# A two-block model step on one core: weights stored as 8 KB rows, TensorE started on zeros, and a re-ordered front

## The reference, cut to what matters

```
h    = rmsnorm(x, g_mix);  proj = h @ w_in              # 1024 x 8208: fox q,k,v | fox_f | sc | dn q,k,v | dn_b | dn_a | z | gates
fox  : 8 heads of 64, q,k normed;  s = q@k^T/8 + cum_f[query] - cum_f[key], causal, softmax, @ v
       cum_f = cumsum(log_sigmoid(fox_f + b_fox_f))
sc   : sb * conv3(sc * sv)
dn   : silu(conv4(dn_qkv)), gated delta rule in chunks of 64, rmsnorm, * silu(z)
x   += (sum_n (y_n @ w_branch[n]) * sigmoid(gate_n)) @ w_o
x   += (silu(conv3(rmsnorm(x) @ w_up)[gate]) * [val]) @ w_down
x   += sigmoid(rmsnorm(x) @ w_ple_gate) * (p @ w_ple)
# second block
x   += concat(diff_attention, pool_mixer) @ ab_w_out ;  x += relu(rmsnorm(x) @ ffn_w1)^2 @ ffn_w2
x   += gated linear attention (gla)                  ;  x += the same kind of ffn again
out  = rmsnorm(x, norm_final)
```

## Time and profile before

| | |
|---|---|
| median of 3 runs | 1150.38 us (1149.55 to 1152.32) |
| the profiled execution | 1149.01 us, of which the span from first to last instruction is 1147.3 |
| PE busy | 1106.8 us, 96% |
| PE weight loads | 980.0 us, 85% |
| DVE, ACT, POOL busy | 67%, 48%, 4% |
| mean granted TensorE clock | 0.990 of full |
| DMA | 185.07 MB, mean 161 GB/s |

### The profile page before, as it was taken

How to read it: one execution, slowest core, us unless ns; L and a number is a source line. 1 busy time by engine, 2 the same in 40 slices (tenths; PEclk the granted TensorE clock), 3 DMA queues, 4 the chain that set the end, 5 groups by cost and what they waited for, 6 DMA issues and landing times.

```text
span 1147.3 us, 17690 instructions
## 1 busy us (share of the span) xinstructions
PE 1106.8 (96%) x7526; PEld 980.0 (85%) x7526; DVE 774.3 (67%) x946; ACT 552.2 (48%) x645; POOL 48.9 (4%) x116
## 2 busy tenths in 40 slices
PE   7899999999999999999998999999999999999996
PEld 6797988998889999998787788888888898888885
DVE  4567688554467998887677576555667876656554
ACT  5457474334446443444664454444454665444442
POOL 8100000000000000000003200000000000000000
PEclk9899899999999999999999999999999999999999
DMA  6776675663355555554553356555635435565551
GB/s 237 185 166 118 111 145 124 138 111 109 103 193 166 189 186 185 191 190 156 182 164 135 120 172 194 186 185 191 197 126 167 129 137 175 183 201 184 184 183 55
DMA packets 128511, 185.07 MB, mean 161 GB/s; under 512 B 6932, under 2 KB 104225, under 8 KB 128434
## 3 DMA queue, kind: packets, MB, share of 16 engines
q1 hardware_dynamic: 123200, 182.46, 53.6%
q10 hardware_dynamic: 4690, 1.36, 0.5%
q0 software_dynamic: 544, 0.13, 0.1%
HBM read 182.89 MB, written 1.05 MB: 160 GB/s over the span
## 4 chain that ended last, share of the span: by engine, by line
PE 82%; DVE 10%; ACT 3%; issue 2%; DMA 2%; SPq 0%; DVEq 0%; ACTq 0%
PE ps L2053 11%; PE ps L2055 10%; PE ps L2068 10%; PE ps L1994 10%; PE ps L2033 9%; PE ps L2039 8%; PE ps L2034 8%; PE ps L2000 5%; DVE low L1344 2%; DMA raw<-in_w_in 2%; DVE arena L1504 1%; PE ps L2083 1%; PE ps L2259 1%; ACT arena L1067 1%; ACT whi L947 0%
## 5 line engine op out<-in xcount | busy, mean ns | idle before, releaser
L947 ACT ACTIVATE whi<-raw 128x2048 fp32r<-128x2048 f32 x170 | 324.0, 1911 | 328.2 <-PE ps L2068 150.7
L1344 DVE TENSOR_TENSOR low<-raw,whi 128x2048 fp32r<-128x2048 f32 x170 | 389.6, 2295 | 56.9 <-ACT whi L947 54.1
L2033 PE MATMUL ps<-hboth,whi 128*128 128x256 f32 x944 | 237.8, 290 | 1.1 <-ACT conv L1043 1.1
L2034 PE MATMUL ps<-hboth,whi 128*128 128x256 f32 x944 | 232.6, 284 | 0.0
L2033 PEld LDWEIGHTS ps<-hboth,whi 128*128 128x128 f32 x944 | 181.6, 192 | 5.9 <-issue 2.9
L2034 PEld LDWEIGHTS ps<-hboth,whi 128*128 128x128 f32 x944 | 182.1, 193 | 0.9 <-issue 0.5
L2053 PE MATMUL ps<-whi,ahi 128*128 128x512 f32 x416 | 164.0, 394 | 4.4 <-issue 2.0
L2055 PE MATMUL ps<-whi,alo 128*128 128x512 f32 x416 | 162.6, 391 | 0.0
L2039 PE MATMUL ps<-hboth,low 128*128 128x256 f32 x944 | 133.3, 284 | 0.3 <-DVE low L1344 0.3
L1994 PE MATMUL ps<-hboth,whi 128*128 128x512 f32 x512 | 128.1, 392 | 0.0
L2039 PEld LDWEIGHTS ps<-hboth,low 128*128 128x128 f32 x944 | 122.6, 193 | 0.5 <-DVE low L1344 0.5
(11 more groups left out here) (393 smaller groups left out, 1222.6 us busy)
## 6 DMA issues: line engine op xcount, KB each, us to landing
raw<-in_ffn_w SPq DMA_DIRECT2D x64, 1024.0 KB, 5.2
raw<-in_w_in SPq DMA_DIRECT2D x30, 1024.0 KB, 10.1
raw<-in_w_up SPq DMA_DIRECT2D x22, 1024.0 KB, 5.1
raw<-in_gla_w_in SPq DMA_DIRECT2D x12, 1024.0 KB, 5.3
raw<-in_w_down SPq DMA_DIRECT2D x11, 1024.0 KB, 4.9
raw<-in_ab_w_in SPq DMA_DIRECT2D x8, 1024.0 KB, 5.2
raw<-in_w_branch SPq DMA_DIRECT2D x6, 1024.0 KB, 5.1
raw<-in_w_o SPq DMA_DIRECT2D x4, 1024.0 KB, 4.9
```

The source lines that it names most:

```text
L947: act.activation(whi[:, u % SPLIT, :], raw[:, u % RAW, :], ACT.Copy).then_inc(sem("hi_done"), 1)
L1344: dve.tensor_tensor(wlo[:, u % RAW, :], raw[:, u % RAW, :], whi[:, u % SPLIT, :].bitcast(F32), ALU.subtract).then_inc(sem("lo_done"), 1)
L2033: pe.matmul(out, wh, hi[:, k0 + k, :], start=opens and k == 0, stop=False, skip_group_check=True)
L2034: pe.matmul(out, wh, lo[:, k0 + k, :], start=False, stop=False, skip_group_check=True)
```

## The change

1. **Layout.** The host now stores every unit as one block of 128 rows of 8 KB (`laid_out`), so a load is 128 rows of 8 KB, contiguous in HBM; the pieces of unit 0 are rows of 2 KB, those of unit 1 rows of 4 KB. SBUF contents are the same.
2. **Parameters.** All per-channel parameters, `g_mix` among them, come as columns in one DMA (128 x 264 f32) on the ACT queue at the start. The 17 POOL DMAs, the memset of their rows, the transposes L2095 and L2109 and the DVE copies out of PSUM are gone. The bias, `dt_bias` and `a_log` rows are one DMA, the small weights another (5 before). p is stored transposed, so the 4 transposes of `ple_p` are gone.
3. **Zeros.** DVE's first instruction clears a 128x128 tile, and PE then multiplies it by itself 12 times (f32) into bank 7 before it waits for anything else.
4. **Gate sums by tile.** `fcum` of the first tile is the gate times (triangle minus 1), that of the second the gate times the triangle: both tiles are counted from the border between them, and the product L2143 is gone. Only differences of the sums are used.
5. **Order.** In the front, `fox(1, 1)` comes before `fox(2, 0)`, the dn units come as 0, 2, 1, 5, 4, 3, and some gates change places; the three tables `steps_at` change. `load_params` issues its 2 DMAs one unit later than before.

```
-    fox(0, 0) fox(0, 1) fox(1, 0) fox(2, 0) dn(0) fox(2, 1) fox(1, 1) dn(5) dn(4) dn(2) dn(1) dn(3)
+    fox(0, 0) fox(0, 1) fox(1, 0) fox(1, 1) fox(2, 0) dn(0) fox(2, 1) dn(2) dn(1) dn(5) dn(4) dn(3)
```

```
-        0: [("load_params", 0)],
-        4: [("load_params", 1)],
-        7: [("params",)],
+        2: [("load_params", 0)],
+        5: [("load_params", 1)],
+        10: [("params",), ("small_split",)],
...
-        15: [("att_norm", 1, 5), ("ab_sum", 0), ("att_turn", 1, 5), ("ab_turn", 0), ("att_values", 1, 4), ("att_values", 1, 5)],
+        15: [("att_norm", 1, 5), ("ab_sum", 0), ("att_turn", 1, 5), ("att_values", 1, 4), ("ab_turn", 0)],
+        16: [("att_values", 1, 5), ("ab_sum", 1)],
...
-        19: [("gla_pairs", 8), ("gla_mask", 8), ("gla_values", 0), ("gla_values", 1), ("gla_sum", 0), ("gla_sum", 1)],
+        19: [("gla_pairs", 7), ("gla_mask", 7), ("gla_pairs", 8), ("gla_mask", 8)],
+        20: [("gla_values", 0), ("gla_sum", 0), ("gla_values", 1)],
...
-                dst = raw[:, u % RAW, :].rearrange("p (k n) -> p k n", k=src.shape[1])
+                src, dst = units[u]["src"], raw[:, u % RAW, :]
...
+    def units(w, rows, cols):
+        r, c = w.shape[0] // rows, w.shape[1] // cols
+        w = w.reshape(r, rows // P, P, c, cols).transpose(0, 3, 2, 1, 4)
+        return w.reshape(r * c, P, UNIT)
...
-                    if t:
-                        lf = zz[:, 3, 0, 4 * b:4 * b + 4].unsqueeze(2).to_broadcast([P, 4, P])
-                        pe.matmul(out, ones[:, :], lf, start=True, stop=False)
-                    pe.matmul(out, ones[:, :], fcum[:, t, 4 * b:4 * b + 4, :], start=t == 0, stop=True)\
+                    pe.matmul(out, ones[:, :], fcum[:, t, 4 * b:4 * b + 4, :], start=True, stop=True)\
...
-                    dve.tensor_tensor(fcum[:, t], wide(tri[:, :].unsqueeze(1), [FH, P]),
-                                      wide(zz[:, 3, t, 0:FH].unsqueeze(2), [FH, P]), ALU.mult)\
+                    dve.scalar_tensor_tensor(out=fcum[:, t], in0=wide(tri[:, :].unsqueeze(1), [FH, P]),
+                                             scalar=-1.0 if t == 0 else 0.0,
+                                             in1=wide(zz[:, 3, t, 0:FH].unsqueeze(2), [FH, P]), op0=ALU.add, op1=ALU.mult)\
...
+            dve.memset(idle, 0.0).then_inc(sem("idle_made"), 1)
...
+            pe.wait_ge(sem("idle_made"), 1)
+            for _ in range(12):
+                pe.matmul(ps[:, 7, 0:P], idle, idle, start=True, stop=True)
```

More of the change, by code:

```diff
@@ L79, in add, with unit_c, unit_w, unit_b @@
         return len(units) - 1
-    def unit_c(w, c0, act, needs):
+    def unit_c(w, act, needs):
         before = [u for u in units if u["kind"] in "CB"]
         bank = 5 if before and before[-1]["kind"] == "C" and before[-1]["bank"] == 4 else 4
[L84 to L97, removed]
+        return add("C", w, act, needs, [f"c{bank}"], bank=bank)
+    def unit_w(w, bank, act, needs):
+        return add("C", w, act, needs, ["c4" if bank == 4 else "c5"], bank=bank, wide=True)
+    def unit_b(w, act, k0, needs, bank, groups):
+        return add("B", w, act, needs, groups, bank=bank, k0=k0)
+    def unit_d(w, act, k0, first, last, needs):
+        return add("D", w, act, needs, ["g0", "g1"], k0=k0, first=first,
                    last=last)
@@ L243, in sc @@
     def sc(e, part):
-        u = unit_c(w_in, o_sc + part * SW + 256 * e, "h", h_ready)
+        u = unit_c(a["w_sc"][SW // 256 * part + e], "h", h_ready)
         if part == 1:
@@ L262, in build @@
     fox(1, 0)
+    fox(1, 1)
     fox(2, 0)
@@ L265, in build @@
     fox(2, 1)
-    fox(1, 1)
+    dn(2)
+    dn(1)
     dn(5)
     dn(4)
-    dn(2)
-    dn(1)
     dn(3)
@@ L279, in build @@
     sc(1, 0)
+    gate(1)
     gate(0)
-    gate(1)
     branch(0, 0, "fox_lo")
@@ L288, in build @@
     branch(1, 0, "sc_lo")
+    gate(6)
     gate(7)
-    gate(6)
     branch(1, 1, "sc_lo")
+    gate(11)
+    gate(8)
+    gate(10)
     gate(9)
-    gate(11)
-    gate(10)
-    gate(8)
     branch(2, 0, "dn_lo")
@@ L419, in build @@
     ab_v()
+    ab_qk(3)
     ab_qk(1)
-    ab_qk(3)
     pool_u(1)
@@ L816, in build @@
         made = {}
-        single = [s[0] for s in order if s[0] in ("norm_first", "params", "dn_square", "dn_cum", "ple_p", "pool_mm")]
+        single = [s[0] for s in order if s[0] in ("dn_square", "dn_cum", "pool_mm")]
         single = {name: 1 + at for at, name in enumerate(single)}
-        loaded = {"gmix": 16, "ple": 32, "pool": 64, "gla": 96, "nfin": 112}
+        loaded = {"columns": 16, "ple": 32, "pool": 64, "gla": 80, "nfin": 96}
         @block.gpsimd
@@ L2470 @@
     arrays, args = {}, {}
-    for name in _INS:
-        v = _np.ascontiguousarray(inputs[name])
+    laid, place = laid_out({name: inputs[name] for name in _INS}, _np)
+    for name, v in laid.items():
+        v = _np.ascontiguousarray(v)
         arrays[f"in_{name}"] = v
@@ L2476 @@
     args["out"] = nc.dram_tensor("out_0", shape, _mybir.dt.from_np(_np.dtype("float32")), kind="ExternalOutput").ap()
-    build(nc, args)
+    build(nc, args, {name: inputs[name].shape for name in _INS}, place)
     r = _run(nc, [arrays], core_ids=[0])
```

329 lines of the change are left out of this document (146 added, 183 removed).

## The result

| | before | after |
|---|---|---|
| median of runs on one chip | 1149.97 us (4 runs, 1148.74 to 1152.32) | 1137.94 us (4 runs, 1133.86 to 1138.11) |
| ratio | | 0.9891, interval 0.9871 to 0.9910 |
| the profiled execution, its span | 1149.01, 1147.3 us | 1137.98, 1136.2 us |
| mean granted clock of that execution | 0.990 | 0.991 |
| runs of both, all chips: span x mean clock | 1136.7 us (54 runs) | 1127.0 us (10 runs) |

What follows compares the result with a forecast made beforehand. PE was taken as the bound, busy 96% of the span. Terms 2.99 + 3.05 + 2.0 + 0.33 + 0.4 - 0.2 + 0.7 + 1.56 gave 10.8 us, so 1150.4 - 10.8 = 1139.6 us; range 1132 to 1145.

Steps and rivals of the forecast that it cites:

- more is won: Rival, chance 0.17: the low clock stretch at 114 to 121 us isn't entered, or 1.7 of gate sums won; 1134 to 1138.
- the clock isn't full to 100 us: Sign of being right: the clock is full from PE's passage from unit 2 to unit 3 up to 100 us.
- the wait ahead of the old L2200: Sign of being right: PE's wait ahead of these thin products has grown to some 2 us.
- Unit order and load: Front, unit 2 to unit 3: PE's wait for ACT goes, 2.99 us, and the clock stays full, 3.05 us.
- The clock, 3.05 of the above: At 33.0 to 39.2 us: with no standstill, 6.1 us of PE work take half as long, 3.05 us won.
- Layout 0: First projection's loads from `w_in`: landing falls from 10.1 to about 5 us, but PE's time gains 0.
- Zeros 2.0: Start: early products raise the clock before the norm products, so ACT's L984 comes 2.0 us earlier.
- Parameters 0.33 + 0.4 - 0.2: Transposes L2109 gone, 0.33 us; transposes of p gone, 0.4; the columns' DMA beside x costs 0.2.
- Gate sums 0: L2143 gone: 1.7 us of PE products, taken as 0 since PE would wait longer for ACT's L1290.
- Tables 0.7 and 1.56: Work moved into PE's waits: 0.7 us at the differential attention's end, 1.56 us ahead of gla's values.
- Other moved steps: All remaining steps whose place in the order changed: between -1 and +1.5 us, taken as 0.
- a gain that shrinks between 60 and 110 us: Sign of being wrong: the front's gain shrinks there, meaning DVE's chain doesn't move with PE.

Runs made afterwards that it cites:

- the second trace: The changed kernel run again, unchanged, for more of its times: 1135.27 us (6 runs), ratio 0.9893.

## Why the prediction was right, and where not

The time was right, and the table by place follows the forecast within 1 us everywhere in the profiled execution. The reasons held less well than the sum, and part of the agreement is luck: in the second trace of the same kernel, with two low stretches fewer, PE is up to 2.2 us further ahead than forecast, and 1137.94 lies also in the 1134 to 1138 of the rival "more is won", of which one half, the gate sums, came true. Of the signs, these failed: the clock isn't full to 100 us, the wait ahead of the old L2200 is gone in place of 2 us, and the stretch between 120 and 560 us gave 1.5 in the second trace in place of 0.4.

*Unit order and load, 2.99 + 3.05:* won at the place as said (6.4 us from start to unit 4 beyond the start's 1.9). But "the order of the units alone wins this; the layout is its insurance" was wrong. Alone, the order wins 6.4 and gives 3 back forty us later, because loads that were hidden by the stall then are waited for, and the clock falls behind that wait. And in the changed kernel neither the order (0.2) nor the rows (0 to 0.9) is needed: without both, 0.55 us of waiting is left. The step that failed is the new start's effect on unit 4's load, put at nothing ("The POOL DMAs were off every chain: 0. ACT issues fewer DMAs in the front"): with the old order and rows, unit 4 lands at 30.0 in the kernel before and at 25.8 with the new start. That this start as a whole does it is shown, and that neither the zeros nor the small weights' rows do it by themselves; the other parameter DMAs are the rival that is left, and that they do it is not shown.

*The clock, 3.05 of the above:* right at 33 to 39 us, but booked as if it were kept. The executions of a kernel differ by some low stretches of 3.4 us, worth 0.3 to 1.5 each by the place. On average over 54 and 10 runs the changed kernel loses 2.4 us less to the clock, not 3.05; the profiled one shows none of it.

*Layout 0:* right, 0 to 0.9. Loads from the same matrix took 9.8 us (median) in old rows and mostly 4.8 to 4.9 in new ones in otherwise one kernel. The rule cited from the Trainium skill, "DMA: Bandwidth & Descriptors", Specifications, says that 512 B are long enough. These runs don't refute it as a rule on length: rows of 1 and 2 KB of this matrix moved 303 GB/s at 95% busy in one window, those of the ffn of 1 and 4 KB land in 5.2 us, and yet rows of 1 KB moved 161 at 90% in another window. So the length of the rows alone doesn't make them slow, and what does stays open. What the rule implied for the time holds, since PE hardly waits for loads.

*Zeros 2.0:* 2.1 to 2.5. Without zeros the clock's first record, at the full level, stands at 10.7, 12.0, 12.2 and 13.4 us in four traces, the first three of the same start. The rule of the Trainium skill, "TensorE: Matmul & The Clock Gate", on warm-up, says that the number of slow matmuls differs from run to run of one kernel; these traces agree. With zeros it comes at 4.0 to 6.3 us in ten traces, always ahead of the norm products, so the scatter falls into products that nobody reads.

*Parameters 0.33 + 0.4 - 0.2:* between the 97th and the 385th product 0.2 are won, p's transposes gave 0.45 by the place. The columns cost 0.2 to 0.6 at the norm products and nearly nothing at unit 0.

*Gate sums 0:* mis-sized, 1.9. I named the cover, ACT's L1290, but read it in the old order of steps. With the new one ACT's L1221 ends at 101.95 (99.96 and 1.99 long in the timeline) and PE begins L2115 at 102.39, right behind the gate sums, so there was nothing left to hide 1.7 us of products. It lay in the rival "more is won".

*Tables 0.7 and 1.56:* 0.9 and 2.05.

*Other moved steps, taken as 0 (-1 to +1.5):* mis-sized in two places, which the clock covered in the first trace. Between the 385th and the 1001st product, 88 and 197 us, PE gains 0.7 there and 1.0 in the second trace. The gate sums give 1.9 of this and the half of the old low stretch that is gone some 1.5 (an estimate, by what the one at 258 cost); the new one at 81 takes 0.3 in the first trace. So the moved steps cost about 2.4; 1.5 of it is seen in PE's waits between 60 and 115 us in the second trace, 5.0 us (1.06, 2.22, 0.46, 1.01, 0.22) against 3.5 before (1.06, 1.49, 0.34, 0.59). That is the sign of a gain that shrinks between 60 and 110 us. Then 1.0 is won near 250 us, where the forecast had no change and the trace of before has a wait of 0.70 that is gone. In sum -1.4, outside of the -1 to +1.5.

So what was forecast too low (gate sums by 1.9, tables by 0.7, zeros by up to 0.5) was nearly cancelled by what was forecast too high (moved steps by some 1.4, the clock behind 60 us). Zeros alone in the old kernel, which won nothing, and the order alone, which kept half, show that the terms were a sum only in this order of edits.

## What to carry to other kernels

A stall covers other lateness: price each edit with the stall there and with it gone, since the zeros here were worth 0 or 2.5 us and the order 3 or 0 by what stood beside them. When a term is costed at nothing, read its cover in the new order of steps, not in the old. Where runs differ by the clock, compare span times mean granted clock: over 54 runs spans that lie 8.7 us apart had a standard deviation of 0.7 in this product. Effects of 2 us show in 4 runs, those of 1 don't; for these take the difference by the place, and look which low stretches each trace has.

## What the runs showed of the hardware

- While PE has work, the clock falls in stretches of 3.4 us (3.4, 6.8 or 10.2). One cost 1.5 us by the place at 258 us, and another 0.3 at 81, where PE waited less behind it. Their places recur (72 to 85, 104 to 122, 254 to 265, 618 to 637, and once 294 to 297, besides the one behind the stall), but which of them a run has differs between executions of one kernel with the same waits. Filling the waits with products didn't raise the mean clock (0.9938 against 0.9933).
- A load can be slow with idle DMA engines: 135 GB/s at 37% busy with a load outstanding, against 303 GB/s at 95% for the same rows in another kernel, which itself has 144 at 49% ten us later. And busy engines can move little: the earlier trace rows has 161 GB/s at 90%. The time to landing alone tells neither apart; the window does.
- Four small DMAs issued in a row took ACT 5.1 us in the run with the small weights in one piece (0.37 for the first, 1.4 to 1.7 for each other), 3.39 of them idle time ahead of the next split:

```profile
22.08 1.65 ACTq L957 DMA_DIRECT2D arena<-in_w_small  x1
...
23.83 1.92 ACT L947 ACTIVATE whi<-raw 128x2048 fp32r<-128x2048 f32 x1 [3.39 <-issue]
```
